# One transpose and two GpSimd transfers per head for the reciprocal softmax sums, and a later split of the gated rows

## The reference, cut to what matters

```
s = einsum('bqhd,bkhd->bhqk', q_i, k) * scale      # then mask / bias
pr = softmax(s, axis=-1)
o  = einsum('bhqk,bkhd->bqhd', pr, v)
mixed = (o * silu(g)) @ w_out
```

## Time and profile before

| | us |
|---|---|
| median of three runs | 1867.72 |
| the profiled execution | 1862.67 |
| its span | 1860.8 |
| PE busy in the span | 1721.7 (93%) |
| DVE busy | 946.8 (51%) |
| ACT busy | 843.1 (45%) |
| POOL busy | 110.2 (6%) |

### The profile page before, as it was taken

How to read it: one execution, slowest core, us unless ns; L and a number is a source line. 1 busy time by engine, 2 the same in 40 slices (tenths; PEclk the granted TensorE clock), 3 DMA queues, 4 the chain that set the end, 5 groups by cost and what they waited for, 6 DMA issues and landing times. The chain is left out here.

```text
span 1860.8 us, 31636 instructions
## 1 busy us (share of the span) xinstructions
PE 1721.7 (93%) x12560; PEld 1604.1 (86%) x12560; DVE 946.8 (51%) x1811; ACT 843.1 (45%) x1714; POOL 110.2 (6%) x65
## 2 busy tenths in 40 slices
PE   5999988999998879999889999999899999899998
PEld 5899987778887769999889999898777777699898
DVE  5554575307787772353455444321177777732531
ACT  4432344417888871231443332322188888712310
POOL 0000000000212210000000000000012122100000
PEclk9999999999999999999999999999999999999999
DMA  5055468526556735101224444343365655251111
GB/s 193 24 172 163 139 165 231 164 87 177 143 141 168 181 90 183 58 29 52 91 91 125 125 131 137 107 131 97 107 162 138 149 138 139 58 193 44 60 63 41
DMA packets 179650, 227.35 MB, mean 122 GB/s; under 512 B 13285, under 2 KB 148725, under 8 KB 179504
## 3 DMA queue, kind: packets, MB, share of 16 engines
q1 hardware_dynamic: 178176, 221.51, 41.6%
q0 software_dynamic: 896, 2.96, 0.6%
q10 hardware_dynamic: 432, 0.85, 0.2%
HBM read 153.42 MB, written 77.63 MB: 124 GB/s over the span
## 5 line engine op out<-in xcount | busy, mean ns | idle before, releaser
L1677 PE MATMUL m_acc<-g_area,g_a_hi 128*128 128x256 f32 (+1 forms) x2560 | 477.6, 287 | 10.1 <-DVE g_area L210 5.6
L1677 PEld LDWEIGHTS m_acc<-g_area,g_a_hi 128*128 128x128 f32 x2560 | 402.8, 192 | 10.4 <-DVE g_area L210 5.7
L1677 PE MATMUL m_acc<-g_area,g_a_lo 128*128 128x256 f32 (+1 forms) x1280 | 365.2, 285 | 0.0
L1677 PEld LDWEIGHTS m_acc<-g_area,g_a_lo 128*128 128x128 f32 x1280 | 244.4, 191 | 0.0
L682 PE MATMUL pa_acc<-g_area,g_a_hi 128*128 128x256 f32 (+2 forms) x1024 | 205.6, 298 | 4.0 <-DVE g_area L210 2.5
L1677 PE MATMUL t_acc<-g_area,g_a_hi 128*128 128x256 f32 x1024 | 190.3, 286 | 5.1 <-DVE g_area L210 5.1
L682 PEld LDWEIGHTS pa_acc<-g_area,g_a_hi 128*128 128x128 f32 x1024 | 165.3, 192 | 4.8 <-issue 2.9
L210 DVE TENSOR_TENSOR g_area<-g_w_raw,g_area 128x2048 fp32r<-128x2048 f32 (+5 forms) x55 | 112.0, 2050 | 111.6 <-ACT g_area L204 111.6
L1677 PEld LDWEIGHTS t_acc<-g_area,g_a_hi 128*128 128x128 f32 x1024 | 161.1, 192 | 5.3 <-DVE g_area L210 5.3
L682 PE MATMUL pa_acc<-g_area,g_a_lo 128*128 128x256 f32 (+2 forms) x512 | 150.8, 295 | 0.0
L1677 PE MATMUL t_acc<-g_area,g_a_lo 128*128 128x256 f32 x512 | 145.9, 285 | 0.0
(11 more groups left out here) (233 smaller groups left out, 3277.2 us busy)
## 6 DMA issues: line engine op xcount, KB each, us to landing
g_w_raw<-in_fox_w_in SPq DMA_DIRECT2D x16, 1024.0 KB, 5.9
g_area<-f_q SPq DMA_DIRECT2D x48, 256.0 KB
g_area<-f_k SPq DMA_DIRECT2D x48, 256.0 KB
g_w_raw<-in_ab_w_in SPq DMA_DIRECT2D x10, 1024.0 KB, 6.0
ab_v<-s_v SPq DMA_DIRECT2D x16, 512.0 KB, 4.3
g_area<-s_q SPq DMA_DIRECT2D x32, 256.0 KB
g_w_raw<-in_pe_gate_w SPq DMA_DIRECT2D x8, 1024.0 KB, 5.2
f_v<-m_pr SPq DMA_DIRECT2D x32, 256.0 KB, 2.6
```

What stands on the lines that cost most here:

```text
L1677: last = nc.tensor.matmul(dst, a[:, k, t * P:(t + 1) * P], w[:, k0 + k, 0:n], start=(k == 0 and a is m_hi and w is w_hi), stop=(k == kt - ...
```

## The change

The reciprocals of a head are taken once, when its eight tiles are done, in one 128 x 8 instruction (`invert`). One transpose (`turn_inverse`) brings them to 8 rows of 128 in `pv`; VectorE copies these rows to SBUF (in `take_o` of the head's last unit). GpSimd's queue writes them to a row of `s_inv` in DRAM, waits for that, and reads the row back to 64 partitions of `far` (`spread_inverse`, 256 KB landing in rows of 1 KB). `take_far` copies the product alone, 64 x 256. The gate's multiplication on GpSimd waits for the transfers. The last head keeps the two transposes for each unit and the 64 x 512 copy. `give` moves from step 9 to step 13 of the pair's sixteen. The transfers of head 14, the last but one, are issued by GpSimd after its loop over the pairs, and VectorE's first `gate_last` waits for them.

```diff
+                    def turn_inverse(hd):
+                        pe.wait_ge(inverted, hd + 1)
+                        nc.tensor.transpose(pv[:, (NU - 1) % 2, 1, 0:P], inverse[:, hd % 2, :], ident[:]).then_inc(inv_turned, 1)
 ...
+                            wait(pe, o_done, uu - 1)
+                            if uu >= NU * (heads - 1):
+                                spread_sums(uu % NU)
+                            elif uu % NU == NU - 1:
+                                turn_inverse(uu // NU)
+                            times_v(uu, False)
 ...
+                        what = slice(0, 2 if last else 1)
+                        nc.scalar.activation(far[64 * b:64 * b + 64, m % 2, u, what], pv[64 - 64 * b:P - 64 * b, uu % 2, what],
                                              ACT.Copy).then_inc(far_done, 1)
 ...
-                        if s % (2 * NT) == 9 and 0 <= m < NPAIR - 1:
+                        if s % (2 * NT) == 13 and 0 <= m < NPAIR - 1:
                             give(m)
 ...
                     def take_o(uu):
 ...
+                        if u == NU - 1 and hd < heads - 1:
+                            dve.wait_ge(pv_done, uu + 1)
+                            dve.wait_ge(inv_turned, hd + 1)
+                            wait(dve, inv_out, 16 * (inv_from + hd - 1))
+                            nc.vector.tensor_copy(inv_rows[:, b, :], pv[0:NT, uu % 2, 1, 0:P]).then_inc(rows_made, 1)
 ...
                     def gate_last(u):
 ...
                             dve.wait_ge(in_g[m % 2], 16 * (m // 2 + 1))
+                            dve.wait_ge(inv_in, 16 * (inv_from + heads - 1))
 ...
+                    def spread_inverse(hd):
+                        b, m = hd % 2, hd // 2
+                        pool.wait_ge(rows_made, hd + 1)
+                        pool.dma_start(s_inv[hd].rearrange("(t q) -> t q", q=P), inv_rows[:, b, :]).then_inc(inv_out, 16)
+                        pool.wait_ge(inv_out, 16 * (inv_from + hd + 1))
+                        wait(pool, gi_done, m - 1)
+                        pool.dma_start(far[64 * b:64 * b + 64, m % 2, :, 1, :],
+                                       s_inv[hd:hd + 1].rearrange("o (u n) -> o u n", u=NU).to_broadcast([64, NU, 2 * P]))\
+                            .then_inc(inv_in, 16)
+
                     for m in range(NPAIR - 1):
+                        spread_inverse(2 * m)
+                        spread_inverse(2 * m + 1)
                         pool.wait_ge(in_g[m % 2], 16 * (m // 2 + 1))
-                        pool.wait_ge(far_done, 2 * NU * (m + 1))
+                        pool.wait_ge(inv_in, 16 * (inv_from + 2 * m + 2))
 ...
                         pool.wait_ge(out_hi, m + 1)
                         nc.gpsimd.tensor_tensor(a_lo[:, m, :], o[:, m % 2, :], a_hi[:, m, :].bitcast(F32), ALU.subtract).then_inc(out_lo, 1)
+                    spread_inverse(heads - 2)
```

More of the change, by code:

```diff
@@ L82, in build @@
     m_ones = dram("m_ones", [3, S])
+    s_inv = dram("s_inv", [FH, S])
     s_bias = dram("s_bias", [HEADS, P, BAND])
@@ L125, in build @@
     pre_qk, pre_w = G.sem("pre_qk"), G.sem("pre_w")
+    inv_out, inv_in = G.sem("inv_out"), G.sem("inv_in")
     qk_area = area[:, 0:8 * S].rearrange("r (b i n) -> r b i n", b=2, i=4)
@@ L965, in stage_ab, with stage_attention @@
             sp.end()
-    def stage_attention(tag, kinds, q_of, k_of, v_of, g_of, extra_of, pre_value, w_next):
+    def stage_attention(tag, kinds, q_of, k_of, v_of, g_of, extra_of, pre_value, w_next, inv_from):
         NT = ST
@@ L1032, in stage_attention @@
             neg_max = sp.sb("neg_max", [P, 4])
-            total = sp.sb("total", [P, 4, 2])
-            inverse = sp.sb("inverse", [P, 4, 2])
+            total = sp.sb("total", [P, 2, NT])
+            inverse = sp.sb("inverse", [P, 2, P])
+            inv_rows = sp.sb("inv_rows", [NT, 2, P])
             scores = sp.ps("scores", [P, 2, S])
@@ L1046, in stage_attention @@
             inverted, spread, pv_done = sp.sem("inverted"), sp.sem("spread"), sp.sem("pv_done")
+            inv_turned, rows_made = sp.sem("inv_turned"), sp.sem("rows_made")
             far_done, gi_done, o_done = sp.sem("far_done"), sp.sem("gi_done"), sp.sem("o_done")
@@ L1119, in turn_p, with spread_sums @@
                             last.then_inc(pieces_turned, 1)
-                    def spread_sums(uu):
-                        wait(pe, o_done, uu - 1)
-                        pe.wait_ge(inverted, uu + 1)
+                    def turn_inverse(hd):
+                        pe.wait_ge(inverted, hd + 1)
+                        nc.tensor.transpose(pv[:, (NU - 1) % 2, 1, 0:P], inverse[:, hd % 2, :], ident[:]).then_inc(inv_turned, 1)
+                    def spread_sums(u):
+                        pe.wait_ge(inverted, heads + u)
                         for i in range(2):
-                            last = nc.tensor.transpose(pv[:, uu % 2, 1, i * P:(i + 1) * P],
-                                                       inverse[:, uu % 4, i:i + 1].to_broadcast([P, P]), ident[:])
+                            last = nc.tensor.transpose(pv[:, u % 2, 1, i * P:(i + 1) * P],
+                                                       inverse[:, (heads - 1) % 2, 2 * u + i:2 * u + i + 1].to_broadcast([P, P]),
+                                                       ident[:])
                         last.then_inc(spread, 1)
@@ L1155, in _ @@
                         if 4 <= s < TILES + 4 and s % 2 == 0:
-                            spread_sums((s - 4) // 2)
-                            times_v((s - 4) // 2, False)
+                            uu = (s - 4) // 2
+                            wait(pe, o_done, uu - 1)
[4 more added lines that the diff above has]
+                            times_v(uu, False)
                 @block.scalar
@@ L1163, in exp @@
                         act.wait_ge(maxed, s + 1)
+                        if t == 0:
+                            wait(act, inverted, s // NT - 1)
                         if not chk:
@@ L1169, in exp @@
                                              scale=-1.0 if chk else 1.0,
-                                             accum_out=total[:, s // 2 % 4, s % 2:s % 2 + 1]).then_inc(exped, 1)
+                                             accum_out=total[:, s // NT % 2, t:t + 1]).then_inc(exped, 1)
                     def evacuate(s):
@@ L1182, in take_far @@
                     def take_far(uu):
-                        b, m = uu // NU % 2, uu // (2 * NU)
+                        b, m, u = uu // NU % 2, uu // (2 * NU), uu % NU
+                        last = uu >= NU * (heads - 1)
                         act.wait_ge(pv_done, uu + 1)
-                        act.wait_ge(spread, uu + 1)
+                        if last:
+                            act.wait_ge(spread, u + 1)
                         if uu % (2 * NU) == 0:
                             wait(act, out_lo, m - 1)
-                        nc.scalar.activation(far[64 * b:64 * b + 64, m % 2, uu % NU], pv[64 - 64 * b:P - 64 * b, uu % 2],
+                        what = slice(0, 2 if last else 1)
+                        nc.scalar.activation(far[64 * b:64 * b + 64, m % 2, u, what], pv[64 - 64 * b:P - 64 * b, uu % 2, what],
                                              ACT.Copy).then_inc(far_done, 1)
@@ L1236, in invert @@
                     def invert(uu):
+                        hd, u = divmod(uu, NU)
+                        b = hd % 2
+                        tiles = slice(0, NT)
+                        if hd == heads - 1:
+                            tiles = slice(2 * u, 2 * u + 2)
+                        elif u < NU - 1:
+                            return
                         dve.wait_ge(exped, 2 * uu + 2)
-                        wait(dve, spread, uu - 3)
-                        nc.vector.reciprocal(inverse[:, uu % 4, :], total[:, uu % 4, :]).then_inc(inverted, 1)
+                        wait(dve, inv_turned, hd - 1)
+                        nc.vector.reciprocal(inverse[:, b, tiles], total[:, b, tiles]).then_inc(inverted, 1)
                     def evacuate(s):
@@ L1274, in give_last @@
                         nc.vector.tensor_tensor(a_lo[:, m, cols], o[:, m % 2, cols], a_hi[:, m, cols].bitcast(F32), ALU.subtract)
+                    nc.vector.memset(inverse[:], 0.0)
                     for s in range(TILES + 6):
@@ L1864, in build @@
                         lambda n: mq(n) if n < HEADS else cq(n - HEADS), lambda n: mk(n) if n < HEADS else ck(n - HEADS),
-                        part(s_v), part(pairs_g), part(s_bias, -HEADS), 16 * QK_LOADS["mla"], ab_w_out[0])
+                        part(s_v), part(pairs_g), part(s_bias, -HEADS), 16 * QK_LOADS["mla"], ab_w_out[0], 0)
         stage_oe("m", 0, ab_w_out[0], x[0].rearrange("(t q) n -> t q n", q=P))
         stage_attention("fox", ["fox"] * FH, split_head(f_q), split_head(f_k), part(f_v), part(pairs_fg), part(s_cum),
-                        16 * (QK_LOADS["mla"] + QK_LOADS["fox"]), fox_w_out[0])
```

(1 more changed line is left out.)

## The result

The changed kernel takes 1880.8 us (median of six runs, 1875.91 to 1883.32); the kernel before, beside it, 1866.64 (six runs). The ratio is 1.0076, 95% interval 1.0059 to 1.0093: slower by 14 us. The forecast was 1881, and +15.6 over the profiled execution of the kernel before.

The account below looks back on a forecast made before the run. Three nearly equally loaded engines, TensorE, ScalarE and VectorE, were taken to wait for one another by turns. Terms -8.5 + 8.8 + 15.3 = +15.6 us on the profiled 1862.67, adjusted towards the runs' median, gave 1881, range 1868 to 1894.

Parts of the forecast that it names:

- parts 1 to 5: Running heads: fewer transposes, shorter far copies and VectorE's changes -8.5 us; give at step 13 +8.8; loop transfers nothing.
- part 6: Ends of both attention stages: VectorE waits for head 14's late transfers; +15.3 us together, bounds 12 and 26.
- Parts 1 to 3: Each head: transposes dropped, far copies shortened, VectorE row copy added; -0.21 us in fox and mla, -0.53 in chk.
- the 0.11 of the transposes: Step 2 of a chk head: a transpose pair out, one transpose in, gains 0.11 us; nothing counted in fox and mla.
- the far copies: ScalarE's copies: 0.21 us less each, two a head on the chain in fox and mla, three in chk.
- the copy: VectorE's new copy of 8 rows from PSUM in step 4, ahead of the sum: costs 0.21 us a head.
- Part 4: Give at step 13, ahead of the chain-opening far copy: adds about 0.96 us each, +8.8 us over twelve pairs.
- Part 5: Transfers in the running loop: GpSimd's first multiplication starts two transfers later, covered by give's late place; costs nothing.
- C: Transposes and far copies in series in every unit through `pv`'s two buffers: -16 us, 1852; chance 0.10.
- B: Ends cost as forecast, but give at step 13 is absorbed and all four far copies count: 1868; chance 0.12.
- D: Transfers at the ends take 5.4 us each, TensorE's drain runs largely at 1.2 GHz: +26 us, 1892; chance 0.13.

Follow-up runs that it names:

- b_give13: The kernel before with only give moved, to step 13 instead of 9: 1881.25 us beside 1865.29 for the kernel before.
- a_order: The changed kernel with head 14's two transfers issued ahead of the low part of the pair before on GpSimd: 1869.93 us, 1.0025 of the kernel before.
- a_lastpair: The changed kernel with both heads of each stage's last pair on the old way, no transfer at the ends: 1869.52 us, 1.0021 of the kernel before.
- b_far: The kernel before with the far copy cut to the product (64 x 256), reciprocals of all but each stage's last head taken as 1: 1851.88 us beside 1865.29.
- b_spread_far: The kernel before with product-only far copies and no transposes but for each stage's first two units and last head, reciprocals there taken as 1: 1854.91 us.
- b_copy: The kernel before with one more VectorE copy a head, 8 rows of 128 from PSUM ahead of step 4's sum, result unused: 1870.85 us.

## Why the prediction was right

- **The sum.** In the two traces the heads between the first and the last of each stage became 1.8 us longer together (the first ones 0.2 shorter), where parts 1 to 5 add up to +0.3; the ends 12.7 us, where part 6 says 15.3. Falls of the clock, which were in no part, add 2.7 to the heads; without them they would be 0.9 us shorter than before. So the ends were put 2.6 us too large and the clock was left out with 2.7; that the total came out so near is in part luck. The mechanisms of parts 4 and 6, which make the change slower, held each by itself (b_give13, a_order, a_lastpair).
- **Parts 1 to 3, a head without a give.** Predicted -0.21 in fox and mla, -0.53 in chk; measured -0.23, -0.40 and -0.48. For fox the terms hold one by one (b_far, b_spread_far, b_copy), and for chk too, but for the 0.11 of the transposes, which isn't there. For mla the sum was half of what came, and its terms were all wrong: there the far copies are worth 0.19 and not 0.42, the transposes 0.28 and not 0, and the copy costs 0.07 and not 0.21. By the code TensorE has three score products a tile in mla, against two in fox, and I take it that it decides more of the cycle there (no run isolates this); I had given mla fox's figures without reading its own timeline.
- **Part 4, give.** Predicted 0.96 a give in step 13; measured 0.92 in fox, 0.88 in mla, 0.95 in chk, and 0.91, 0.92 and 0.96 in b_give13. Over the twelve pairs, less what give cost before, that is 8.7 us; parts 1 to 3 bring 10.3. The price before held too (0.07 in fox, 0.68 in chk; in mla it was nothing, which I had taken like fox).
- **Not foreseen:** TensorE at 1.2 GHz behind some gives, 0.8 to 1.0 us each, three times in the profiled execution, about 2.7 us in all. I had counted the clock only at the ends.
- **Part 5.** GpSimd's first multiplication of a fox pair starts 17 to 18 us after the exp of the pair's last tile, against 10.1 before: 7 to 8 us later, as said, and give waits for nothing. What it leads to, that give needn't wait until step 13 in mla and fox, I did not see. Nine gives of mla and fox at about 0.9 us, 8 us together, hung on it, and so did the falls of the clock behind some of them.
- **Part 6.** Predicted D = 6.6 us for both transfers; measured 5.57 in fox (1626.43 to 1632.00) and 5.99 in ab (683.20 to 689.19), of which the 4 KB write took 1.85 and 1.90 and not 2.7. This is the term that was too large, by 1.6 us in both ends together; where the other microsecond lies that part 6 had too much is open. (The working also has 1620.6 where its terms give 1620.5.) The rule of the Trainium skill ("DMA: Bandwidth & Descriptors", "Anatomy of one DMA — SWDGE (gpsimd) path") would have had 4.6, so its fixed 2.0 us fits the write here, and the broadcast back with 3.72 is a microsecond over its 2.6. The waits were 5.45 and 5.86, together 11.3; a_order and a_lastpair take off 9 to 12.
- **The rivals.** C (faster, all in series over `pv`) needed 0.8 us for far copies and again 0.8 for transposes in every head; fox shows 0.42 and nothing. B needed give absorbed and all four far copies on the path; b_give13 shows 0.91 for give, b_far two copies. D needed transfers of 10.8 us.

## What to carry to other kernels

An instruction that is nearly free in one step of a software pipeline can be almost wholly exposed four steps on: in fox give cost 0.07 us in step 9 and 0.92 in step 13. When work is handed to a slow queue, moving other steps to cover its latency can cost nearly all that the change brings (here 8.7 us of some 10); read when the result is really there, and put the consumer back to the first hidden place behind it. And look at the last iteration by itself: what a queue does in order behind other work was hidden here in every round but the last, whose result is wanted at once.

## What the runs showed of the hardware

- The same 4 KB write on GpSimd's queue took 1.83 to 1.90 us to the next issue in fox and at the ends of both stages when little else was moving (DMA share 0.01 to 0.11), and 4.8 to 4.9, in ab up to 7.3, while the loads for the coming heads were under way (share 0.86 to 1.06). GpSimd in fox after the change:

```profile
1591.75 0.56 POOL L1332 DMA_DIRECT2D s_inv<-fox_inv_rows  x1
1596.68 0.66 POOL L1335 DMA_DIRECT2D fox_far<-s_inv  x1 [4.38 <-DMA s_inv<-fox_inv_rows]
```

- TensorE's clock fell behind some of several like pauses: after waits of 0.99 and 1.07 us one behind the other it was 0.56 in the one head and 1.00 two heads on. What chose between them no run here shows.
